# Parameter vectors loaded as rows and turned by one transpose, products of high parts one granule ahead in the first unit, the second half of x in two loads

## What is computed

```python
xn = rmsnorm(x, norm_mix[l])
p = xn @ w_in[l]
pA, pB, pC, pD = jnp.split(p, [A_COLS, A_COLS + B_COLS, A_COLS + B_COLS + C_COLS], axis=-1)
yA = rwkv7_mixer(pA, rwkv_mu[l], rwkv_w0[l], rwkv_w2[l], rwkv_a0[l], rwkv_a2[l],
                 rwkv_g2[l], rwkv_k_k[l], rwkv_k_a[l], rwkv_r_k[l],
                 rwkv_gn_w[l], rwkv_gn_b[l])
...
    p = p + (shift_right(p) - p) * mu
```

## Time and profile before

| | |
|---|---|
| median of 3 runs | 975.29 us (975.19 to 976.81) |
| the profiled execution | 975.61 us |
| its span in the profile | 973.8 us |
| around the span | 1.8 us |
| PE busy | 951.4 us (98%) |
| DVE busy, ACT busy, POOL busy | 437.8, 282.2, 79.9 us |
| moved by DMA | 285.83 MB, mean 294 GB/s |

### The profile page before, as it was taken

How to read it: one execution, slowest core, us unless ns; L and a number is a source line. 1 busy time by engine, 2 the same in 40 slices (tenths; PEclk the granted TensorE clock), 3 DMA queues, 4 the chain that set the end, 5 groups by cost and what they waited for, 6 DMA issues and landing times.

```text
span 973.8 us, 18328 instructions
## 1 busy us (share of the span) xinstructions
PE 951.4 (98%) x8110; PEld 741.2 (76%) x8110; DVE 437.8 (45%) x693; ACT 282.2 (29%) x458; POOL 79.9 (8%) x87
## 2 busy tenths in 40 slices
PE   8999999999999999999999999999999999999994
PEld 8999999999999999988877656565665656566551
DVE  5657947443656567675443132231414232241404
ACT  6455543232236566545530010100100010010104
POOL 6010003132000000520000000000000000000002
PEclk9999999999999999999999999999999999999998
DMA  9795543233344444699988999999999999999993
GB/s 287 204 286 164 160 129 126 86 94 123 108 125 140 141 138 132 238 306 403 337 336 351 412 395 428 428 427 427 427 427 426 429 427 424 428 428 426 427 404 136
DMA packets 83122, 285.83 MB, mean 294 GB/s; under 512 B 3868, under 2 KB 55288, under 8 KB 69728
## 3 DMA queue, kind: packets, MB, share of 16 engines
q1 hardware_dynamic: 80896, 279.98, 74.4%
q0 software_dynamic: 1824, 4.04, 1.7%
q10 hardware_dynamic: 320, 0.60, 0.2%
HBM read 280.39 MB, written 4.22 MB: 292 GB/s over the span
## 4 chain that ended last, share of the span: by engine, by line
PE 82%; DMA 6%; DVE 5%; ACT 3%; issue 2%; SPq 1%; POOL 0%; DVEq 0%; ACTq 0%; POOLq 0%
PE bank L972 22%; PE bank L1371 22%; PE bank L1393 9%; PE bank L1341 5%; DMA arena<-in_expert_w_gate 4%; PE bank L989 3%; PE bank L991 3%; PE bank L990 3%; DMA arena<-in_w_in 2%; PE bank L917 2%; DVE ring_r L1574 2%; PE bank L1351 1%; PE bank L1412 1%; PE bank L1352 1%; PE bank L1091 1%
## 5 line engine op out<-in xcount | busy, mean ns | idle before, releaser
L972 PE MATMUL bank<-xTr,hi 128*128 128x256 f32 x1344 | 249.1, 287 | 2.1 <-DVE ring_r L1574 2.0
L1371 PE MATMUL bank<-arena 128*64 128x256 f32 x2048 | 229.4, 380 | 0.7 <-DMA arena<-in_expert_w_gate 0.5
L1574 DVE TENSOR_TENSOR ring_r<-arena,hi 128x1024 fp32r<-128x1024 f32 x132 | 163.6, 1251 | 132.6 <-ACT hi L629 130.8
L972 PEld LDWEIGHTS bank<-xTr,hi 128*128 128x128 f32 x1344 | 208.8, 191 | 8.7 <-issue 4.5
L1371 PEld LDWEIGHTS bank<-arena 128*64 128x64 f32 x2048 | 146.0, 137 | 78.4 <-issue 10.8
L972 PE MATMUL bank<-xTr,ring_r 128*128 128x256 f32 x672 | 189.9, 283 | 0.0
L629 ACT ACTIVATE hi<-arena 128x1024 fp32r<-128x1024 f32 x132 | 138.6, 1060 | 112.0 <-PE bank L972 77.4
L972 PEld LDWEIGHTS bank<-xTr,ring_r 128*128 128x128 f32 x672 | 128.6, 191 | 0.0
L1393 PE MATMUL bank<-arena,const 128*64 128x512 f32 x448 | 100.8, 597 | 0.0
L1992 DVE TENSOR_TENSOR arena<-arena,bank 128x512 f32<-128x512 f32 x60 | 63.9, 1111 | 40.5 <-PE bank L1352 40.5
L1393 PEld LDWEIGHTS bank<-arena,const 128*64 128x64 f32 x448 | 30.3, 137 | 54.5 <-issue 52.0
(11 more groups left out here) (331 smaller groups left out, 945.6 us busy)
## 6 DMA issues: line engine op xcount, KB each, us to landing
arena<-in_expert_w_up SPq DMA_DIRECT2D x30, 2048.0 KB, 22.5
arena<-in_expert_w_gate SPq DMA_DIRECT2D x29, 2048.0 KB, 24.3
arena<-in_w_in SPq DMA_DIRECT2D x50, 1024.0 KB, 5.3
arena<-in_expert_w_down SPq DMA_DIRECT2D x24, 2048.0 KB, 22.9
arena<-in_w_out SPq DMA_DIRECT2D x16, 1024.0 KB, 8.0
arena<-in_expert_w_down SPq DMA_DIRECT2D x14, 1024.0 KB, 13.1
arena<-in_expert_w_gate SPq DMA_DIRECT2D x6, 1024.0 KB, 7.7
arena<-in_expert_w_up SPq DMA_DIRECT2D x4, 1024.0 KB, 8.8
```

Source lines behind the costliest of these rows:

```text
L972: ins = MM(PJ[n % 2][:, h * U:(h + 1) * U], a, b, start=h + q + tt + k == 0, stop=h == 1 and q == 3 and tt == 3 and k == 2)
L1371: ins = MM(bank[7 if last and st_ else 2 + st_][CAP * a:CAP * a + CAP, c // 2 * U:(c // 2 + 1) * U], xg[:, t, CAP * a:CAP * a + CAP], slot ...
L1574: TT(ring_r[:, n % 2, q, :], ring[:, n % 2, q, :], hi[:, g % NHI, :].bitcast(f32), ALU.subtract).then_inc(s["lo_done"], 1)
```

## The change

- All eight vectors (`norm_mix`, `mu`, `w0`, `a0`, `k_k`, `k_a`, `r_k`, `conv_w`) are loaded by ACT as rows of 128, 62 rows in all, in eight DMAs at the start. One transpose turns them, and one copy brings them to SBUF. POOL's seven loads of columns are gone.
- x of m = 1 comes in two loads of 1024 columns each. DVE squares the first when it has landed, and the fourth quarter. ACT squares the third quarter only.
- `x_high`/`x_low` of pairs 0 and 1 now stand ahead of granule 0's split, and so on for granules 1 and 2.
- In unit 0, PE does the eight products high by high of a granule apart from the other sixteen, in the order high 0, high 1, low 0, pair 7 of x, high 2, low 1, high 3, low 2, low 3.
- ACT loads the rest of `const` behind `keep(0)`, and the high part of granule 7 now stands ahead of the tanh. DVE's preparation of `mu`, `w0`, `a0` and `k_a` moves ahead of `x_low`. POOL's copy of `before` moves behind the loads of the biases.

```diff
-        xs, xsq, gain1, diag = at(112, NM, DM), at(128, NM, DM), at(144, KT), at(144.25, NM, P)
-        gain_nat = at(145.5, P)[0:KT, :]
+        NVEC = KT + 14 + 5 * AT + 3 * AT
+        xs, xsq, diag = at(112, NM, DM), at(128, NM, DM), at(144.25, NM, P)
+        vec_nat = at(145.5, P)[0:NVEC, :]
...
+        vec, omu, ok_a = sb("vec", [P, NVEC]), sb("omu", [P, 14]), sb("ok_a", [P, AT])
+        vec_at = 0
+
+        def next_vec(n):
+            nonlocal vec_at
+            vec_at += n
+            return vec[:, vec_at - n:vec_at]
+        gain1, mu = next_vec(KT), next_vec(14)
+        w0h, a0h, k_k, k_a, r_k = (next_vec(AT) for _ in range(5))
+        cw = next_vec(3 * AT).rearrange("p (j t) -> p j t", j=3)
...
-            for m in range(NM):
-                sp.dma_start(xs[:, m, :], x_v[m]).then_inc(x_ld[m], 16)
+            sp.dma_start(xs[:, 0, :], x_v[0]).then_inc(x_ld[0], 16)
+            for n, part in ((1, slice(0, DM // 2)), (2, slice(DM // 2, DM))):
+                sp.dma_start(xs[:, 1, part], x_v[1][:, part]).then_inc(x_ld[n], 16)
...
-        NPAR = 17
+        NPAR = 11
+        NVECS = 8
...
-                (w0h[:, :], cols(A["rwkv_w0"])), (a0h[:, :], cols(A["rwkv_a0"])),
-                (k_k[:, :], cols(A["rwkv_k_k"])), (k_a[:, :], cols(A["rwkv_k_a"])),
-                (r_k[:, :], A["rwkv_r_k"].rearrange("l (t e) k -> (e k) (l t)", e=2)),
...
-                (cw[:, :, :], A["conv_w"].rearrange("l j (t p) -> p (l j) t", p=P)),
...
-            pool.dma_start(mu[:, :], cols(A["rwkv_mu"])).then_inc(par2_ld, 16)
...
-            act.dma_start(gain_nat, A["norm_mix"].rearrange("l (t p) -> (l t) p", p=P)).then_inc(gain_ld, 16)
+            vectors = [as_rows(A[n]) for n in ("norm_mix", "rwkv_mu", "rwkv_w0", "rwkv_a0", "rwkv_k_k", "rwkv_k_a")]
+            vectors += [A["rwkv_r_k"].rearrange("l (t e) k -> (l t) (e k)", e=2),
+                        A["conv_w"].rearrange("l j (t p) -> (l j t) p", p=P)]
+            row = 0
+            for src in vectors:
+                act.dma_start(vec_nat[row:row + src.shape[0], :], src).then_inc(gain_ld, 16)
+                row += src.shape[0]
+            assert row == NVEC and len(vectors) == NVECS
             act.wait_ge(x_ld[0], 16)
             step(A_(xsq[:, 0, :], xs[:, 0, :], ACT.Square, accum_out=st[:, 0:1]), s["sq1_done"])
-            act.wait_ge(x_ld[1], 16)
-            step(A_(xsq[:, 1, 0:DM // 2], xs[:, 1, 0:DM // 2], ACT.Square, accum_out=st[:, 2:3]), s["sq1_done"])
-            act.wait_ge(s["diag0_done"], 1)
-            act.dma_start(const[:, P:], A["const"][:, P:]).then_inc(const_ld, 16)
-            act.wait_ge(gain_ld, 17)
-            A_(gain1, PJ[0][:, 0:KT], ACT.Copy).then_inc(gain_ld, 1)
-            act.wait_ge(gain_ld, 18)
+            act.wait_ge(gain_ld, 16 * NVECS + 1)
+            A_(vec[:, :], PJ[0][:, 0:NVEC], ACT.Copy).then_inc(gain_ld, 1)
+            act.wait_ge(x_ld[2], 16)
+            third = slice(DM // 2, DM // 2 + 512)
+            step(A_(xsq[:, 1, third], xs[:, 1, third], ACT.Square, accum_out=st[:, 2:3]), s["sq1_done"])
+            act.wait_ge(gain_ld, 16 * NVECS + 2)
...
             for b in range(8):
-                if b % 2 == 0 and b < 2 * LEAD:
+                x_high(b)
+                if b % 2 == 1 and b < 2 * LEAD:
                     split_hi()
-                x_high(b)
             advance(4)
             keep(0)
+            act.dma_start(const[:, P:], A["const"][:, P:]).then_inc(const_ld, 16)
+            advance(1)
             act.wait_ge(s["mixA"], 2)
             step(A_(mA[0:64, 12, :], mA[0:64, 12, :], ACT.Tanh), s["tanhA"])
             step(A_(mA[:, 13, :], mA[:, 13, :], ACT.Tanh, scale=0.5), s["tanhA"])
-            advance(4)
+            advance(3)
...
-            pe.wait_ge(gain_ld, 16)
-            nc.tensor.transpose(PJ[0][:, 0:KT], gain_nat, ident[0:KT, 0:KT]).then_inc(gain_ld, 1)
+            pe.wait_ge(gain_ld, 16 * NVECS)
+            nc.tensor.transpose(PJ[0][:, 0:NVEC], vec_nat, ident[0:NVEC, 0:NVEC]).then_inc(gain_ld, 1)
             warm(26)
             pe.wait_ge(s["diag0_done"], 1)
             for b in range(7):
                 x_transpose(b, 0)
             pe.wait_ge(s["diag1_done"], 1)
-            for b in range(8):
-                if b == 7:
-                    pe.wait_ge(s["xlo_done"], 2)
-                    x_transpose(b, 0)
+            for b in range(7):
                 x_transpose(b, 1).then_inc(s["xt_ready"], 1)
 
-            pos = {"g": 0}
+            def first_high(q):
+
+                wh = hi[:, q, :].rearrange("p (t c) -> p t c", t=4)
+                pe.wait_ge(s["hi_done"], q + 1)
+                pe.wait_ge(s["xhi_done"], 4 * q + 4)
+                if q == 0:
+                    pe.wait_ge(gain_ld, 16 * NVECS + 2)
+                for h in range(2):
+                    for tt in range(4):
+                        MM(PJ[0][:, h * U:(h + 1) * U], wh[:, tt, h * P:(h + 1) * P], xTr[:, 0, 4 * q + tt, :],
+                           start=h + q + tt == 0, stop=False)
+
+            def first_low(q):
+
+                wh = hi[:, q, :].rearrange("p (t c) -> p t c", t=4)
+                wl = ring_r[:, 0, q, :].rearrange("p (t c) -> p t c", t=4)
+                pe.wait_ge(s["xlo_done"], 4 * q + 4)
+                for w, a in ((wh, 1), (wl, 0)):
+                    if a == 0:
+                        pe.wait_ge(s["lo_done"], q + 1)
+                    for h in range(2):
+                        for tt in range(4):
+                            ins = MM(PJ[0][:, h * U:(h + 1) * U], w[:, tt, h * P:(h + 1) * P], xTr[:, a, 4 * q + tt, :],
+                                     start=False, stop=q == 3 and a == 0 and h == 1 and tt == 3)
+                ins.then_inc(s["gran_used"], 1)
+
+            first_high(0)
+            first_high(1)
+            first_low(0)
+            x_transpose(7, 0)
+            x_transpose(7, 1).then_inc(s["xt_ready"], 1)
+            first_high(2)
+            first_low(1)
+            first_high(3)
+            first_low(2)
+            first_low(3)
+            pos = {"g": 4}
 
             def in_granule(n, q):
-                if n == 0:
-                    pe.wait_ge(s["xlo_done"], 4 * q + 4)
-                elif q == 0 and n >= 2:
+                if q == 0 and n >= 2:
...
-            granules(8)
+            granules(4)
...
-            v.wait_ge(x_ld[1], 16)
-            half = slice(DM // 2, DM)
-            step(V.tensor_tensor_reduce(xsq[:, 1, half], xs[:, 1, half], xs[:, 1, half], 1.0, 0.0, ALU.mult, ALU.add, st[:, 1:2]))
+            for n, part in ((1, slice(0, DM // 2)), (2, slice(DM // 2 + 512, DM))):
+                v.wait_ge(x_ld[n], 16)
+                step(V.tensor_tensor_reduce(xsq[:, 1, part], xs[:, 1, part], xs[:, 1, part], 1.0, 0.0, ALU.mult, ALU.add,
+                                            st[:, 2 * n - 1:2 * n]))
+            step(TT(st[:, 1:2], st[:, 1:2], st[:, 3:4], ALU.add))
             v.wait_ge(s["sq1_done"], 2)
             step(TT(st[:, 1:2], st[:, 1:2], st[:, 2:3], ALU.add))
             variance(1)
             v.wait_ge(const_ld, 16)
             v.wait_ge(s["rstd_done"], 2)
             step(TS(diag[:, 1, :], ident, st[:, 1:2], None, ALU.mult), s["diag1_done"])
+            v.wait_ge(gain_ld, 16 * NVECS + 2)
+            step(TS(omu[:, :], mu, -1.0, 1.0, ALU.mult, ALU.add), s["prep"])
+            step(TS(w0h, w0h, 0.5, None, ALU.mult), s["prep"])
+            step(TS(a0h, a0h, 0.5, None, ALU.mult), s["prep"])
+            step(TS(ok_a[:, :], k_a, -1.0, 1.0, ALU.mult, ALU.add), s["prep"])
...
             for b in range(8):
-                if b % 2 == 0 and b < 2 * LEAD:
+                x_low(b)
+                if b % 2 == 1 and b < 2 * LEAD:
                     split_lo(1)
-                x_low(b)
-            split_lo(2)
-            v.wait_ge(par2_ld, 16)
-            step(TS(omu[:, :], mu[:, :], -1.0, 1.0, ALU.mult, ALU.add), s["prep"])
-            split_lo(2)
+            split_lo(4)
             mix(0)
-            v.wait_ge(const_ld, 32)
+            split_lo(1)
             v.wait_ge(par_ld, 16 * NPAR)
-            step(TS(w0h[:, :], w0h[:, :], 0.5, None, ALU.mult), s["prep"])
-            step(TS(a0h[:, :], a0h[:, :], 0.5, None, ALU.mult), s["prep"])
-            step(TS(ok_a[:, :], k_a[:, :], -1.0, 1.0, ALU.mult, ALU.add), s["prep"])
```

More of the change, by code:

```diff
@@ L183, in build @@
         th = g2[:, :].rearrange("p (s n) -> p s n", s=2)
-        cw = sb("cw", [P, 3, AT])
         lam = sb("lam", [P, 8])
@@ L226, in build @@
         t5_dram = nc.dram_tensor("t5_scratch", [4, SPAN], f32)
-        x_ld = [sem(f"x_ld{m}") for m in range(NM)]
+        x_ld = [sem(f"x_ld{m}") for m in range(NM + 1)]
         gain_ld, par_ld, par2_ld, par3_ld, const_ld = (sem(n) for n in ("gain_ld", "par_ld", "par2_ld", "par3_ld", "const_ld"))
@@ L314, in cols, with as_rows @@
             return v.rearrange("l (t p) -> p (l t)", p=P)
+        def as_rows(v):
```

(8 more changed lines are left out.)

5 lines of the change are left out of this document (removed).

## The result

| | before | after |
|---|---|---|
| median of 7 runs each | 975.29 us | 979.34 us |
| lowest to highest | 974.35 to 977.45 | 979.16 to 982.0 |
| ratio | | 1.0045 [1.0035, 1.0055] |
| the profiled execution, its span | 975.61, 973.8 us | 981.3, 979.4 us |

The change costs 4.05 us. The forecast was 977.6 us. Of the times on record, that of rival B (978.9) is the nearest.

What follows compares the result with a forecast made beforehand. PE was taken as the bound, with a shift at its start reaching the end one for one. Order and granule 7 +0.55 plus later start +1.8 gave +2.35 us, put against the 975.3 median: 977.6 us, range 975.6 to 980.2.

Steps and rivals of the forecast that it cites:

- rival B: At the start, PE's clock falls during its wait, slowing small products and some turns: +1.2 to +1.7, 978.9; chance 0.20.
- steps 1 and 2: Unit 0's new order makes PE wait for granule 1's high part, +1.5 us; granule 7's wait goes, -0.95; together +0.55.
- Step 3: At the start, PE waits for the last vector, landing at 9.5 us; turns of x begin at 11.4, +1.8 us.
- Step 4: Earlier squares of m=1, the 62-column copy, DVE's four small instructions and POOL's copy near the start cost nothing.
- Rival C: ACT's small loads are served in turn with SP's large ones; last vector at some 20 us, 988 us; chance 0.11.
- Rival A: Vectors land earlier, 6.8 to 9.1 us, or the order costs less: +0.75 to +1.95, 976.6, not slower; chance 0.31.
- Rival D: Faster by over 0.2%, which would need 2 us from places where PE does not wait; chance 0.04.

Runs made afterwards that it cites:

- with the clock held: The changed kernel with 112 small products ahead of the transpose instead of 52, nothing else: 978.19 us, 1.0030.
- the squares apart: Changed kernel with the old order, vectors' transpose behind m=0's seven pairs, 105 small products ahead, DVE's m=1 squares held until m=0's `diag`: 975.86 us, 1.0003.

## Why the prediction was off

**What bounds the kernel, steps 1 and 2.** Right. The new order brought the wait ahead of high 1: high 0 starts at 19.47 and has work for 0.96 us at 0.12 a product, high 1 starts at 21.88, which is 1.45 us without work (1.4 predicted; the profile's row says 1.19, since it models PE's last product as running on). In all the order costs 1.6 us against 1.5. Granule 7's wait is gone in after, because its weight lands at 26.1 instead of 31.27. That makes +0.55 predicted for both, +0.7 measured in after and with the clock held. With the order alone it is +1.0, since a part of the wait is left there.

**Step 3.** Right, and by the right row. Issue of the last vector 4.19 (4.4 predicted), landing 9.60 (9.5), turns at 11.63 (11.4). `norm_mix`'s 5.4 us in the earlier trace rows held for the last of the eight vectors, in the same queue. Of the 2.0 us, 0.25 is the clock: the 26 small products. The fixed 2 us for one DMA that the Trainium skill gives ("DMA: Bandwidth & Descriptors", section "Anatomy of one DMA") did not come true here: 5.41 us in after, 5.34 with ten loads, both under the load of x and weights.

**Step 4.** One term failed: "cost nothing" for the squares of m = 1. DVE's earlier square made POOL's power 0.9 us longer and `diag` ready at 10.6 instead of 9.56. It lay under the wait for the vectors in after, so the sum did not suffer. It made the kernel with the late transpose late by 0.9 us at the yardstick (42.13, and 41.22 with the squares apart). The trace of before shows no DVE instruction beside a POOL instruction in this stretch, so the cost of putting one there had no row.

**The sum.** +2.35 us predicted, +4.07 measured. The step that failed is the choice between the forecast and rival B: the clock was given a chance of 0.20 to fall and stood in the sum at nothing. It fell, at a cost of 1.6 us (1.4 in the turns, 0.25 in the small products), inside the +1.2 to +1.7 that the rival gave. The reason against it was that PE was busy right up to the idle time. The row for it was the earlier trace rows, the only idle time of this length in the trace, and the clock fell there, though after PE's last work. A row of the same length should have weighed more than the reason.

**Rival C** is false. The eight issues of ACT took 0.26 to 0.67 us each, none of the four weight issues grew past 4.25 us (3.78 before), and the vectors came at 9.6 and not at 20. The Trainium skill says that SP and ACT have no descriptor generator of their own ("DMA: Bandwidth & Descriptors", section "Queues, rings and completion order"). That may well hold; these traces show that it does not make small loads wait in turn behind long ones. **Rival A** asked for a landing before 9.1 or a cheaper order, and is false: the landing came 0.5 us later, and the order cost 1.6 us. **Rival D** has nothing for it.

The range, 975.6 to 980.2, held the time, and the side (slower by over 0.2%) was right. The range held because its upper end priced rival B. The forecast's own account, with the clock at 1.00 throughout, would have been 1.7 us short.

## What to carry to other kernels

- A vector that becomes a wait for PE costs twice: the wait, and then PE's clock, if it falls. Here the second was 1.6 us of 4.1. Small products that lasted until the data were there took it away, at no cost in the timeline.
- Work of DVE with two inputs in SBUF was not free beside POOL. Before an instruction is moved earlier, look at what POOL does at that time, even if no semaphore ties the two.
- Gathering seven tiny loads into rows for one transpose saved POOL's queue work that nobody waited for, and put its cost on ACT's queue and PE, where someone did. The one part worth taking moved 512 KB out from among the weights, and even its 0.8 us at the yardstick is too little to be told in the median.

## What the hardware did that was not expected

- **POOL waits for the end of DVE's instruction.** Its power went from 0.57 to 1.51 and 1.60 us, the making of `diag` from 0.61 to 1.46, each ending 0.4 to 0.5 us after DVE's square.
- **The clock's fall is not decided by the length of the idle time alone.** In the kernel before with the added square PE was idle for 2.94 us and the clock stayed:

```profile
11.52 7.41 PE L933 MATMUL bank<-arena 128*128 128x128 f32 x64 [2.94 <-POOL arena L487]
```

  In the kernel with the first split ahead of x it was idle for 2.62 us and the clock fell:

```profile
9.76 0.24 PE L956 MATMUL bank<-const,arena 62*128 62x62 f32 x1 [2.62 <-DMA arena<-in_conv_w]
```

  (There it fell at 10.7, with PE at work again.) The 2.21 us without work ahead of the last 16 products are in both before and after, and the clock stayed at 1.00 in the one and fell at 963.4 in the other. At 3.79, 3.92 and 4.04 us it fell in each of the three traces, at 8.1, 11.1 and 8.8, and stayed low for 6.8, 3.4 and 6.8 us. So one kernel's cost can't be carried to the next to better than a factor of two. The Trainium skill ("TensorE: Matmul & The Clock Gate", section "Part 1: The HAM clock gate") says that the chip's watch on PE's activity runs free and does not begin with the kernel. That would fit different times of the fall in kernels with the same start, but no run here moved the start against it. What PE did ahead of the idle time differs too: the 52 small products took 5.73 us in the kernel where the clock fell at 2.62, 0.11 each, which is the pace of the 26 at a clock of 0.50 (2.96 us), and 5.37 in the one where it stayed. What decides between 2.62 and 2.94 stays open.
- **Landing times of tiny loads follow their issue at a nearly fixed distance.** It is 5.2 to 5.5 us beside the loads of x and weights: 5.4 for the second load of ACT's queue (before), 5.24 to 5.50 for the ninth in four traces with eight vectors, 5.34 for the eleventh with ten. Each one more adds only its issue.
